# Two fused transformer blocks: the first operand pair behind each norm by the chunk, and the modulation's SiLU behind the first weight roundings

## What is computed

```python
def swiglu_ffn(x, w_gate_up, w_down):
    gu = x @ w_gate_up                       # 1024 x 5632
    gate, up = gu[..., :2816], gu[..., 2816:]
    return (silu(gate) * up) @ w_down

for i in range(2):                           # first block
    h = even_mixer(x, ...) if i == 0 else odd_mixer(x, ...)
    x = layer_norm(ALPHA * x + h, ln_g[i, 0], ln_b[i, 0])
    x = layer_norm(ALPHA * x + swiglu_ffn(x, ...), ln_g[i, 1], ln_b[i, 1])

mod = silu(c) @ w_ada + b_ada                # second block, w_ada 1024 x 6144
sh1, sc1, g1, sh2, sc2, g2 = split(mod, 6)
h = rmsnorm(x, g[0]) * (1 + sc1) + sh1
x = x + g1 * rmsnorm(token_mixer(h, ...), g[1])
h = rmsnorm(x, g[2]) * (1 + sc2) + sh2
x = x + g2 * rmsnorm(square(relu(h @ w1 + b1)) @ w2 + b2, g[3])
```

## Time and profile before

| | |
|---|---|
| time, median of 3 runs | 1136.97 us (1131.41 to 1138.66) |
| profiled execution, its own time | 1133.92 us |
| its span / outside it | 1131.8 us / 2.1 us |
| TensorE busy | 1071.9 us (95%) |
| VectorE / ScalarE / POOL busy | 64% / 46% / 12% |
| granted TensorE clock, mean | 0.976 |
| moved by DMA | 193.67 MB, 171 GB/s |

### The profile page before, as it was taken

How to read it: one execution, slowest core, us unless ns; L and a number is a source line. 1 busy time by engine, 2 the same in 40 slices (tenths; PEclk the granted TensorE clock), 3 DMA queues, 4 the chain that set the end, 5 groups by cost and what they waited for, 6 DMA issues and landing times.

```text
span 1131.8 us, 16907 instructions
## 1 busy us (share of the span) xinstructions
PE 1071.9 (95%) x7008; PEld 944.4 (83%) x7008; DVE 721.4 (64%) x1004; ACT 518.6 (46%) x742; POOL 134.8 (12%) x151
## 2 busy tenths in 40 slices
PE   7999999987999999899897999999799999999998
PEld 7888998877999988676676999988688778999886
DVE  4597863686776666677746676675755657666443
ACT  4452432354444343456645344443455656555332
POOL 2044841024000000500005000000200000000000
PEclk9899999898999999999999999999999998999999
DMA  9531011265786786336933886777353323555550
GB/s 301 162 104 57 1 39 38 76 222 189 259 297 216 259 305 224 131 123 148 202 113 103 299 283 221 242 290 272 100 184 115 112 75 106 187 185 186 193 186 38
DMA packets 113597, 193.67 MB, mean 171 GB/s; under 512 B 4690, under 2 KB 85089, under 8 KB 113394
## 3 DMA queue, kind: packets, MB, share of 16 engines
q1 hardware_dynamic: 109986, 180.18, 47.7%
q0 software_dynamic: 3248, 11.83, 4.8%
q10 hardware_dynamic: 288, 0.59, 0.1%
HBM read 188.39 MB, written 4.19 MB: 170 GB/s over the span
## 4 chain that ended last, share of the span: by engine, by line
PE 80%; DVE 10%; ACT 5%; DMA 3%; issue 2%; POOL 1%; DVEq 0%; SPq 0%; ACTq 0%; POOLq 0%
PE ps L444 22%; PE ps L446 21%; PE ps L445 21%; DMA ring<-in_ffn_w_gate_up_dram 2%; DVE ARR L400 2%; PE ps L2139 2%; PE ps L1281 2%; PE ps L1296 2%; PE ps L2124 2%; ACT ARR L387 1%; PE ps L2117 1%; DVE XL L602 1%; DVE AR L1218 1%; PE ps L1547 1%; PE ps L1504 1%
## 5 line engine op out<-in xcount | busy, mean ns | idle before, releaser
L400 DVE TENSOR_TENSOR ARR<-ring,ARR 128x2048 fp32r<-128x2048 f32 (+2 forms) x140 | 313.6, 2245 | 195.6 <-ACT ARR L387 195.5
L444 PE MATMUL ps<-XH,ARR 128*128 128x256 f32 x1240 | 356.0, 287 | 16.4 <-DVE ARR L400 6.6
L387 ACT ACTIVATE ARR<-ring 128x2048 fp32r<-128x2048 f32 (+2 forms) x141 | 263.5, 1875 | 200.6 <-PE ps L446 141.4
L445 PE MATMUL ps<-XL,ARR 128*128 128x256 f32 x1240 | 352.6, 284 | 0.0
L446 PE MATMUL ps<-XH,ARR 128*128 128x256 f32 x1240 | 352.3, 284 | 0.0
L444 PEld LDWEIGHTS ps<-XH,ARR 128*128 128x128 f32 x1240 | 237.6, 192 | 23.7 <-issue 19.0
L445 PEld LDWEIGHTS ps<-XL,ARR 128*128 128x128 f32 x1240 | 237.8, 192 | 0.5 <-issue 0.2
L446 PEld LDWEIGHTS ps<-XH,ARR 128*128 128x128 f32 x1240 | 237.5, 192 | 0.1
L444 PE MATMUL ps<-ARR 128*128 128x512 f32 x420 | 167.7, 399 | 5.0 <-DVE ARR L400 2.0
L446 PE MATMUL ps<-ARR 128*128 128x512 f32 x420 | 165.9, 395 | 0.0
L445 PE MATMUL ps<-ARR 128*128 128x512 f32 x420 | 165.8, 395 | 0.0
(11 more groups left out here) (352 smaller groups left out, 1236.3 us busy)
## 6 DMA issues: line engine op xcount, KB each, us to landing
ring<-in_ffn_w_gate_up_dram SPq DMA_DIRECT2D x44, 1024.0 KB, 5.8
ring<-in_w_dram SPq DMA_DIRECT2D x32, 1024.0 KB, 5.1
ring<-in_w_ada_dram SPq DMA_DIRECT2D x24, 1024.0 KB, 5.3
ring<-in_ffn_w_down_dram SPq DMA_DIRECT2D x22, 1024.0 KB, 5.1
ring<-in_even_w_in_dram SPq DMA_DIRECT2D x13, 1024.0 KB, 5.7
ring<-in_w_in_dram SPq DMA_DIRECT2D x9, 1024.0 KB, 5.3
ring<-in_mla_w_q_b_dram SPq DMA_DIRECT2D x6, 768.0 KB, 4.1
ring<-in_even_w_out_dram SPq DMA_DIRECT2D x4, 1024.0 KB, 4.9
```

Source lines behind the costliest of these rows:

```text
L387: e.activation(split(i)[0], raw(i), ACT.Copy).then_inc(*up("hi", ("hi", i)))
L400: e.tensor_tensor(lo, raw(i), hi.bitcast(F32), ALU.subtract).then_inc(*up("lo", ("lo", i), ("raw free", i)))
L444: e.matmul(out, lhs[0], rhs[0], start=first, stop=False)
L445: e.matmul(out, lhs[0], rhs[1], start=False, stop=False)
```

## The change

Four things are edited.

1. `act_scaled`: where pair 0 is concerned, ScalarE first rounds its two chunks one at a time, each as soon as VectorE has scaled it. Only then does it scale pair 1. The pair's single rounding goes.
2. `dve_scaled`: each chunk of pair 0 is announced after its scaling; then VectorE takes the remainder of chunk 0 and that of chunk 1 by themselves.
3. `pe_pair` starts with chunk 0 alone, then chunk 1, then pairs as before; `pe_rows` has a form `by_chunk`, used at n1, cq and m0, in which the first weights meet the first 128 tokens chunk by chunk.
4. `act_ffn`: `act_modulation_start` moves from the function's start to behind the two split calls of j = 0.

```diff
@@ -450,10 +450,10 @@
             b = [bank(e, tag), bank(e, (tag, "second"))]
             hilo = split(w)
             e.wait_ge(*at(("lo", w)))
-            for c in range(0, 8, 2):
-                e.wait_ge(*at(xready(c // 2)))
+            for part in ((0,), (1,), (2, 3), (4, 5), (6, 7)):
+                e.wait_ge(*at((*xready(0), 0) if part == (0,) else xready(part[0] // 2)))
                 for h in range(2):
-                    for c_ in (c, c + 1):
+                    for c_ in part:
                         k = mm3(e, b[h][:, h * 256:h * 256 + 256], cut(hilo, ALL, c_, slice(h * P, h * P + P)),
                                 cut(xT, ALL, c_), c_ == 0, c_ == 7)
             return k
@@ -482,7 +482,8 @@
         def parts_of(n):
             return [(o, min(512, n - o)) for o in range(0, n, 512)]
 
-        def pe_rows(e, tag, kc, n, xT, xready, begun=False, between=None, tail=1):
+        def pe_rows(e, tag, kc, n, xT, xready, begun=False, between=None, tail=1,
+                    by_chunk=False):
 
 
             parts = parts_of(n)
@@ -501,6 +502,16 @@
                     if between and k0 in between:
                         between[k0](e)
                     e.wait_ge(*at(("lo", w, 0) if w == gate else ("lo", w)))
+                if by_chunk and t == k0 == 0:
+
+                    for c in range(k0, k1):
+                        e.wait_ge(*at(xready(c // 2) if c else (*xready(0), 0)))
+                        for j, (o, m) in enumerate(parts):
+                            if c == 0 and before[t, j] is not None:
+                                e.wait_ge(*at(("free", before[t, j])))
+                            mm3(e, ps((tag, t, j))[:, 0:m], cut(xT, ALL, c, slice(0, P)),
+                                cut(hilo, ALL, c - k0, slice(o, o + m)), c == 0, False)
+                    continue
                 for j, (o, m) in enumerate(parts):
                     if k0 == 0 and before[t, j] is not None:
                         e.wait_ge(*at(("free", before[t, j])))
@@ -555,10 +566,19 @@
                     *up("rest", ("xt", use), ("free", use)))
 
 
+
         def tf_half(v):
             return TF[:, v, :].rearrange("p (c t) -> p c t", c=2)
 
         def act_scaled(e, tag, dst, scale, shift, before, tf_before, part=(0, 1)):
+            if 0 in part:
+                for i in range(2):
+                    e.wait_ge(*at(("scaled", (tag, 0), i)))
+                    if i == 0:
+                        for step in before:
+                            e.wait_ge(*at(step))
+                    e.activation(dst[0][:, i, :], tf_half(0)[:, i, :], ACT.Copy).then_inc(
+                        *up("first", ("first", (tag, 0), i)))
             for c in (2 + 4 * n for n in part):
                 use = (tag, c // 2)
                 e.wait_ge(*at(("full", use)))
@@ -572,12 +592,9 @@
                     else:
                         k = e.activation(y, x, ACT.Identity, bias=shift(c + i), scale=scale(c + i))
                 k.then_inc(*up("first", ("scaled", use), ("free", use)))
-                for v in range(2):
+                for v in range(1 if c == 2 else 0, 2):
                     use = (tag, c // 2 - 1 + v)
                     e.wait_ge(*at(("scaled", use)))
-                    if c == 2 and v == 0:
-                        for step in before:
-                            e.wait_ge(*at(step))
                     e.activation(dst[0][:, c - 2 + 2 * v:c + 2 * v, :], tf_half(v), ACT.Copy).then_inc(
                         *up("first", ("first", use)))
 
@@ -594,8 +611,16 @@
                         k = e.tensor_scalar(y, x, scale(c + i), None, ALU.mult)
                     else:
                         k = e.tensor_scalar(y, x, scale(c + i), shift(c + i), ALU.mult, ALU.add)
-                k.then_inc(*up("rest", ("scaled", use), ("free", use)))
-                for v in range(2):
+                    if c == 0:
+                        k.then_inc(*up("rest", ("scaled", use, i), *([("free", use)] if i else [])))
+                if c == 0:
+                    for i in range(2):
+                        e.wait_ge(*at(("first", use, i)))
+                        e.tensor_tensor(dst[1][:, i, :], tf_half(0)[:, i, :], dst[0][:, i, :].bitcast(F32), ALU.subtract
+                                        ).then_inc(*up("rest", ("xt", use) if i else ("xt", use, 0)))
+                if c:
+                    k.then_inc(*up("rest", ("scaled", use), ("free", use)))
+                for v in range(0 if c else 1, 2):
                     use = (tag, c // 2 + v)
                     hi, lo = (x[:, c + 2 * v:c + 2 * v + 2, :] for x in dst)
                     e.wait_ge(*at(("first", use)))
@@ -1818,11 +1843,12 @@
             pe_norm(e, i) if i < 3 else None
 
         def act_ffn(e, layer, i):
-            act_modulation_start(e, layer)
             for j in range(0, 22, 2):
                 u = UP[:, (j // 2) % 2, :]
                 for g in range(2):
                     act_split(e, ahead(("gu", layer, j, g), 0))
+                if j == 0:
+                    act_modulation_start(e, layer)
                 tag = ("gu", layer, j, 0)
                 e.wait_ge(*at(("full", tag)))
                 if j >= 4:
@@ -1904,11 +1930,11 @@
                         ).then_inc(*up("pos", "positions", by=16))
 
         def pe_mla_projections(e):
-            pe_rows(e, "min", 8, 1024, XT, xt_step("n1"), tail=2)
+            pe_rows(e, "min", 8, 1024, XT, xt_step("n1"), tail=2, by_chunk=True)
             pe_rope_key(e)
             pe_transposed(e, "cq", CQ, 8, lambda t: [("cq", t)])
             pe_rope_key_rows(e)
-            pe_rows(e, "mqb", 6, 1536, CT, xt_step("cq"))
+            pe_rows(e, "mqb", 6, 1536, CT, xt_step("cq"), by_chunk=True)
             pe_bias(e)
             for half in range(2):
                 pe_rows(e, f"mkv{half}", 2, 1024, cut(CT, ALL, slice(6, 8)), lambda c: ("xt", ("cq", 3)))
@@ -2417,7 +2443,7 @@
                 k.then_inc(*up("products", ("used", w), ("full", use)))
 
         def pe_in2(e):
-            pe_rows(e, "va2", 8, 512, XT, xt_step("m0"))
+            pe_rows(e, "va2", 8, 512, XT, xt_step("m0"), by_chunk=True)
             for i in (0, 2):
                 for part in range(4):
                     pe_in2_quarter(e, i, part)
```

## The result

The changed kernel took 1152.46 us (median of 4 runs, 1150.99 to 1156.93) beside 1136.2 for the kernel before on the same chip: ratio 1.0174, 95% interval 1.0144 to 1.0204. The loss is then some 20 us, not 16. The profiled execution is the slowest of the four, 1156.93 us with a span of 1154.8. Some 2.4 us of its distance to the profile of before had already come up when the transposes of n0 began (259.99 against 257.60), ahead of everything that was edited, so what follows compares stretches, not moments.

The account below looks back on a forecast made before the run. It took TensorE's waits for the first operand pair after each of six norms as the bound. 7.3 (layer 0) + 7.0 (layer 1) + 0.95 (chunks) = +15.25 us gave 1149.2 or 1152.2, stated as 1151, range 1143 to 1159.

Parts of the forecast that it names:

- The SiLU behind E: Feed-forward start: SiLU waits for weights E, VectorE's piece C for the SiLU, D behind C; +7.3 us layer 0, +7.0 layer 1.
- E's landing: Weight load E, issued earlier and without F competing, lands at 275.3 in layer 0 and 627.6 in layer 1.
- The clock's loss: TensorE behind the new stall ahead of D: 4.2 us at the low clock lose 1.9 us per layer, bounds 0 and 2.9.
- What it gives back: TensorE's earlier stalls ahead of E, G and J vanish: 2.4 us in layer 0, 1.75 and 1.05 in layer 1.
- The chunks: Pair 0 a chunk at a time at six norms: earlier first products, longer engine chains; together +0.95 us, bounds -4 and +2.
- m1: At this norm first products start at 942.4 instead of 943.69; -0.5 us, bounds -1.3 and 0.
- cq and m0: At these two places products start 1.0 and 1.25 us earlier, but later VectorE work holds TensorE: +0.7 and +0.4 us.
- n1: At this norm the start gains nothing, and the VectorE chain ahead of the next weights is 0.35 us longer: +0.35.
- Rival 1: Short stall: E lands after 5.0 us in both layers and the clock loses nothing; +7.6, 1143 us; chance 0.12.
- rival 4: The stall travels: E keeps its 7.4 and 8.9 us landing, G is 1 to 2 us late per layer; +20, 1156; chance 0.06.
- 2: Not slower: SiLU runs before E's rounding, so VectorE is not held; -1.6, 1135 us (1129 with every chunk gain); chance 0.04.
- 3: ScalarE drains for about 1.28 us at each moved table load, on the path twice; +17.8, 1154 us; chance 0.04.

Follow-up runs that it names:

- run 6: Changed kernel with POOL's four loads of each layer held until weight piece J has landed: 1146.16 us, ratio 1.0128 to the kernel before.
- run 2: Changed kernel with the SiLU back at the start of act_ffn, so only the chunk-wise pair 0 remains: 1134.58 us, ratio 1.0023 to the kernel before.
- run 4: Changed kernel with the SiLU between the two split calls of j = 0, pair 0 still chunk-wise: 1134.49 us, ratio 1.0024 to the kernel before.
- run 5: Changed kernel with VectorE's first split call taking B, D, C instead of B, C, D: 1149.47 us, ratio 1.0147 to the kernel before.
- run 10: Changed kernel with the SiLU between the split calls and POOL's loads held until J has landed, chunks kept: 1128.61 us, ratio 0.9955.
- run 3: Kernel before with the SiLU between the two split calls of j = 0, no chunks: 1133.13 us, ratio 1.0005.
- run 8: Kernel before with SiLU between split calls, POOL's loads held, CSL in its own columns and no SiLU of c in layer 1: 1128.26 us, ratio 0.9958.
- run 1: Kernel before with the SiLU behind both split calls of j = 0, no chunks: 1152.55 us, ratio 1.0185.
- run 7: Kernel before with the SiLU between the split calls and POOL's loads held until J has landed: 1125.48 us, ratio 0.9944.
- run 9: Kernel before with only POOL's four loads of each layer held until J has landed: 1130.22 us, ratio 0.9970.

## Why the prediction was right

It said 1151 in a range of 1143 to 1159 and slower by over 1% at 0.82; 1152.46 came, and 1.74%. That the time came within 1.5 us is in part luck: the sum was +15.25 on a base taken between 1133.9 and 1137.0, and the loss was some 20 on a base of 1132.7. The interval, 16 to 23 us, lies wholly over the sum. The mechanism was right; its size was some 4.5 us short, and the lines below say where the profile has more than the sum.

**The SiLU behind E.** Every step shows in the rows: E, table load, SiLU, C, D, and the idle SyncE queue. By stretches, from the last transposes of n0 to those of n1 the changed kernel took 209.36 us and the kernel before 201.22, +8.1 against a forecast of +7.3; from n2 to m0 216.8 against 207.9, +8.9 against +7.0. D's products started 1.4 and 2.4 us later than forecast, counted from the transposes (27.0 and 28.7 in place of 25.6 and 26.3). The term that was mis-sized is E's landing. I let it end by 275.3 and 627.6 by a count of bytes; it ended 19.0 us after n0's transposes (forecast 17.7) and 20.7 after n2's (18.4). The earlier issue and the absence of F together brought E in only 0.5 and 0.7 us earlier, counted from the transposes: it landed 7.7 and 9.7 us after its issue (7.4 and 8.9 before), and run 6, where it took 5.1 and 6.4, shows that POOL's loads have their part in it. Both landings lie behind even the upper bounds of the forecast (275.9 and 629.2, which is 18.3 and 20.0 us after the transposes). The clock's loss was a little smaller than worked out (3.3 us at the low level, not 4.2).

**What it gives back.** Right: the stalls ahead of E, G and J are gone.

**The chunks.** The sum of +0.95 stands beside +2 measured in run 2, within its interval (0.3 to 4.9). In single places:

- Measured from the place's transposes, first products came earlier at all six in the changed kernel's profile: by 0.9 us at n0 and cq, 1.3 at n1, 1.6 at n2, 1.2 at m0, but only 0.6 at m1 (0.3 to 0.7 in the six kernels with chunks), where 1.3 was forecast.
- cq and m0 went as worked out. The first row below is cq's first product, the second its wait for a bank; then the same of m0, with its wait for the next weights:

```profile
506.09 0.47 PE L444 MATMUL ps<-ARR 128*128 128x512 f32 x1 [0.64 <-issue]
...
511.33 0.50 PE L444 MATMUL ps<-ARR 128*128 128x512 f32 x1 [1.51 <-DVE TF L611]
...
842.78 0.77 PE L444 MATMUL ps<-ARR,XH 128*128 128x512 f32 x1 [0.37 <-issue]
...
852.05 0.50 PE L444 MATMUL ps<-ARR,XH 128*128 128x512 f32 x1 [0.93 <-DVE ARR L400]
```

  The bank comes 7.21 us after the transposes (6.58 before: +0.63, forecast +0.7), m0's weights after 11.61 (11.11: +0.5, forecast +0.4).
- At n1 the forecast was a start that stays and a VectorE chain that is 0.35 longer, and neither holds in every profile. The first product came 2.22 us after the transposes in the changed kernel and in run 2, 1.0 to 1.3 earlier than without chunks (3.19 to 3.48), but in the four other kernels with chunks it came at 3.55 to 3.91. The next weights came after 12.00 or 12.01 us in the changed kernel and in runs 2 and 4, no later than without chunks (11.99 to 12.01), with a remainder of pair 1 of 0.69 us in place of the 0.97 reckoned with; in runs 5, 6 and 10 it took 1.2, and they came after 12.16 to 12.24.

**The rivals.** 1 and 4 are sizes of the same stall, and the truth lies between the forecast and rival 4, whose first half (E keeps its landing) is what happened; G was not late. 2 falls by the rows of the changed kernel; in runs 3 and 4 its condition was made true, and the loss was gone, though the 1.6 us that it forecast under the kernel before did not come. (Rival 1's sum takes 2.1 us off in layer 1 where its own times give 2.3; that changes nothing.) 3 falls: the table load begins 0.02 us after E's rounding, and the SiLU at its end. That is against the drain in the Trainium skill's page "ScalarE: Activation LUTs", section "What ACT_TABLE_LOAD costs", and with its figure for the load (1.28).

**What the sum left out.** From n1 to n2 the changed kernel's profile is 3.9 us longer than that of before (154.3 and 150.4), where 1.05 was forecast. 0.6 of it is the edit at cq: TensorE's next long wait ends 37.4 to 37.5 us after cq's transposes in all six kernels with chunks, and after 36.8 in the six without. The rest is the place and the number of stretches of low clock. One of them is in the changed kernel and in run 2 alone (the changed kernel, then the kernel before, the same place behind cq):

```profile
543.50:545.50 2.00, 2.00 (x6) 1.56 (x5) 2.00 (x2) 0.52 (x2) 0.00 (x0) 0.50 0.90 94
...
530.80:532.80 2.00, 2.00 (x10) 1.63 (x9) 2.00 (x2) 1.06 (x4) 0.00 (x0) 1.00 0.85 90
```

What decides where they fall is open; the last section has what the twelve profiles show.

## What to carry to other kernels

Before a short operation is moved behind others on its engine, look at what the last of them waits for: here the new place was behind a load, and the operation's own 1.5 us became 9 and 12 us of stall. Follow its reader through every queue that is served in order, the engine's and the DMA issuer's; taking the waiting piece out of one of them (run 5) won back only a sixth. And when an earlier start buys nothing, ask which transfer lands last: it was only when loads that nobody needed yet were put off that the kernel got faster. And the next wait that was taken away (run 8) let another transfer out earlier, and the one that was needed came later.

## What the runs showed beyond that

**A stretch of low clock moves rather than goes.** The stretches between the transposes of n1, cq and n2, in us, in the profiles of all twelve kernels, with the number of stretches of low clock (down to a granted 0.50) that were not hidden. One is hidden where TensorE would have had to wait behind those products anyway.

| profiles | n1 to cq | cq to n2 | low and not hidden |
|---|---|---|---|
| before, run 3 | 33.2 | 117.2, 117.3 | 1, behind cq |
| runs 1, 7, 8, 9 | 34.7 to 34.8 | 115.7 to 115.8 | 1, behind n1 |
| run 4 (chunks) | 33.2 | 116.3 | 0 |
| run 5 (chunks) | 33.4 | 118.0 | 1, behind cq |
| runs 6, 10 (chunks) | 35.0 | 116.6, 116.3 | 1, behind n1 |
| changed, run 2 (chunks) | 34.8, 34.7 | 119.5 | 3, one behind n1, two behind cq |

The six kernels without chunks take 150.4 to 150.6 us for the whole, however the first part went. Each low stretch that is not hidden costs about 1.5 us. The kernels with chunks have none to three of them and take 149.5 to 154.3; with one profile of each kernel, whether the chunks have a part in that number is not shown. Nor is it shown that other edits have none: all five kernels with POOL's loads held are among those with 34.7 to 35.0, and three of the other seven.

Windows of the kernel before, of the changed one, and of run 7: first the 6 us from the transposes on, then the 4 us behind the wait for the next weights. The column in front of the last two is the granted clock.

```profile
458.00:464.00 6.00, 5.18 (x16) 3.01 (x17) 4.51 (x7) 3.41 (x7) 5.92 (x8) 0.72 0.00 0
...
470.80:474.80 4.00, 3.99 (x17) 3.25 (x18) 4.00 (x2) 0.10 (x1) 0.00 (x0) 1.00 0.70 198
```

```profile
469.00:475.00 6.00, 5.65 (x25) 4.14 (x26) 4.28 (x8) 3.74 (x8) 5.92 (x8) 1.00 0.01 3
...
481.40:485.40 4.00, 4.00 (x11) 3.19 (x12) 4.00 (x2) 0.00 (x0) 0.00 (x0) 0.57 0.69 206
```

```profile
453.00:459.00 6.00, 5.01 (x22) 3.36 (x23) 4.28 (x7) 3.39 (x8) 5.92 (x8) 1.00 0.01 3
...
465.60:469.60 4.00, 4.00 (x11) 3.14 (x12) 4.00 (x2) 0.00 (x0) 0.00 (x0) 0.57 0.80 208
```

In the first of the three the low stretch falls on the products ahead of the wait, where it is hidden, and TensorE then idles 1.93 us. In the other two those products run at 2.4 GHz (granted 1.00), the idle time is 3.0 and 3.6 us, and the 4 us behind it are granted 0.57. Runs 6 and 10 have a low stretch on both sides of the wait. I had been ready to put these 1.5 us on the chunks; the run of the SiLU alone has them, the run with chunks and the SiLU between does not.

**Landing times.** The same 1 MB load of E, from issue to landing, took 7.4 to 9.1 us in layer 0 and 8.9 to 9.8 in layer 1 with 2.1 MB of POOL's issued just ahead, and 5.0 to 5.2 and 6.4 to 7.3 with these held. In layer 1 the 6.4 us were there with F 3.2 us behind E (run 7) and with F 12 us behind it (run 6), so F does not explain them; what does was not tried.
